# A blocked triangular inverse inside a two-block transformer kernel: corner products, narrower updates, masks on another engine

## What is computed

```python
decay = jnp.exp(jnp.where(causal, gc[..., :, None] - gc[..., None, :], -jnp.inf))
a_strict = jnp.where(idx[:, None] > idx[None, :],
                     jnp.einsum('bhncd,bhnsd->bhncs', k_beta, k) * decay, 0.0)
tri = a_strict + jnp.eye(c)
u = triangular_solve(tri, v * beta[..., None], lower=True, unit_diagonal=True)
w = triangular_solve(tri, k_beta * jnp.exp(gc)[..., None], lower=True, unit_diagonal=True)
```

## Time and profile before

| | us |
|---|---|
| median of 3 runs | 2701.99 |
| lowest, highest | 2698.80, 2703.09 |
| the profiled execution, its own time | 2697.01 |
| its span, first to last instruction | 2695.2 |
| PE busy, share of the span | 91% |
| DVE busy | 65% |
| ACT busy | 42% |
| POOL busy | 4% |
| mean granted PE clock, 1 is 2.4 GHz | 0.957 |

### The profile page before, as it was taken

One profiled execution on the slowest core, in us unless ns is written; L12 is line 12 of the kernel. 1 busy time (PEld: TensorE's weight loads), 2 busy tenths in 40 slices (PEclk: granted clock), 3 DMA queues, 4 the chain that ended last, 5 costly groups with the idle time before them and its releaser, 6 DMA issues. The chain is left out here.

```text
span 2695.2 us, 46289 instructions
## 1 busy us (share of the span) xinstructions
PE 2464.9 (91%) x18937; PEld 2367.2 (88%) x18937; DVE 1739.8 (65%) x2529; ACT 1120.7 (42%) x1600; POOL 103.2 (4%) x149
## 2 busy tenths in 40 slices
PE   6788679997986799989998999999999989999998
PEld 6788569997965699989998889899999988898998
DVE  4765357776383477757775575677777755756776
ACT  4542343333463333324334655533433346554332
POOL 2300000000000000000003000000000030000000
PEclk8999779998998699999999999999999999999999
DMA  7320135553911355534556223455364463234542
GB/s 198 122 79 17 35 109 188 187 187 105 221 43 51 104 177 180 180 109 164 180 172 161 94 95 110 157 172 187 131 197 162 151 172 99 94 119 163 180 162 80
DMA packets 294979, 370.17 MB, mean 137 GB/s; under 512 B 15321, under 2 KB 263634, under 8 KB 294802
## 3 DMA queue, kind: packets, MB, share of 16 engines
q1 hardware_dynamic: 289584, 354.85, 40.4%
q0 software_dynamic: 4880, 13.13, 2.7%
q10 hardware_dynamic: 370, 0.11, 0.0%
HBM read 360.20 MB, written 7.86 MB: 137 GB/s over the span
## 5 line engine op out<-in xcount | busy, mean ns | idle before, releaser
L302 PE MATMUL psum_banks<-source_high,weights_high 128*128 128x272 f32 (+1 forms) x3680 | 1080.4, 294 | 71.8 <-DVE weights_low L1540 21.3
L304 PE MATMUL psum_banks<-source_high,weights_low 128*128 128x272 f32 (+1 forms) x3680 | 1065.2, 289 | 0.0
L303 PE MATMUL psum_banks<-source_low,weights_high 128*128 128x272 f32 (+1 forms) x3680 | 1065.1, 289 | 0.0
L302 PEld LDWEIGHTS psum_banks<-source_high,weights_high 128*128 128x128 f32 x3680 | 710.6, 193 | 82.8 <-issue 24.3
L303 PEld LDWEIGHTS psum_banks<-source_low,weights_high 128*128 128x128 f32 x3680 | 711.2, 193 | 0.7
L304 PEld LDWEIGHTS psum_banks<-source_high,weights_low 128*128 128x128 f32 x3680 | 710.1, 193 | 0.0
L302 PE MATMUL psum_banks<-hidden_high,weights_high 128*128 128x272 f32 (+1 forms) x1216 | 349.8, 288 | 0.2 <-DVE h L1039 0.2
L304 PE MATMUL psum_banks<-hidden_high,weights_low 128*128 128x272 f32 (+1 forms) x1216 | 348.4, 287 | 0.0
L303 PE MATMUL psum_banks<-hidden_low,weights_high 128*128 128x272 f32 (+1 forms) x1216 | 347.3, 286 | 0.0
L1540 DVE TENSOR_TENSOR weights_low<-weight_ring,weights_high 128x2048 fp32r<-128x2048 f32 x102 | 234.1, 2297 | 174.0 <-ACT weights_high L1533 173.4
L1013 DVE TENSOR_TENSOR weights_low<-weight_ring,weights_high 128x2048 fp32r<-128x2048 f32 x131 | 292.9, 2287 | 74.0 <-ACT weights_high L1007 73.9
(11 more groups left out here) (403 smaller groups left out, 2902.8 us busy)
## 6 DMA issues: line engine op xcount, KB each, us to landing
weight_ring<-ffn_w_in SPq DMA_DIRECT2D x88, 1024.0 KB, 6.6
weight_ring<-w_in SPq DMA_DIRECT2D x48, 1024.0 KB, 5.3
weight_ring<-ffn_w_out SPq DMA_DIRECT2D x44, 1024.0 KB, 5.0
weight_ring<-moe_w_gate SPq DMA_DIRECT2D x32, 1024.0 KB, 6.8
weight_ring<-moe_w_up SPq DMA_DIRECT2D x32, 1024.0 KB, 7.6
weight_ring<-moe_w_down SPq DMA_DIRECT2D x32, 1024.0 KB, 5.0
weight_ring<-gdn_w_in SPq DMA_DIRECT2D x16, 1024.0 KB, 5.9
weight_ring<-w_branch SPq DMA_DIRECT2D x12, 1024.0 KB, 5.1
```

The costliest lines, as they stand in the source:

```text
L302: pe.matmul(out, w_hi, x_hi, start=start, stop=False)
L303: pe.matmul(out, w_hi, x_lo, start=False, stop=False)
L304: return pe.matmul(out, w_lo, x_hi, start=False, stop=stop)
```

## The change

Three edits are made in `gdn_layer`, all in the inverse.

1. In levels 0 to 4 a product of eight heads is made by `per_block`: for each head two products of 64x64 with 64 columns, one in rows and columns 0 to 63, one in rows and columns 64 to 127 of the array. Up to blocks of 64 nothing else of the 128x128 matrices is used. The last level keeps the full products.
2. DVE updates only what a level changes: in X the left block of each pair of blocks, in XT the right one, for each corner apart. This is four instructions on 64 partitions with 256 elements each, in place of two with 128x1024. The last level updates only columns 64 to 127 of XT, 128x512.
3. The masked matrices `pair` of levels 1 to 5 are made by POOL, and not by DVE between the products. They alternate between two pairs of buffers: levels 0, 2 and 4 use `temp`, levels 1, 3 and 5 use `spare`, which lies in `squares` and `raw`. POOL's mask for level 1 waits for the turned matrix of its chunk (the same event as `first(t)`), the masks for level 2 on wait until the first product of the level two before has been made. PE waits for `ready` before each first product from level 1 on.

```diff
-        half_step, pair = (A[:, 0], A[:, 1]), (temp[:, 0], temp[:, 1])
+        half_step = (A[:, 0], A[:, 1])
+        spare = [ap.rearrange("p n c -> p (n c)")[:, 0:H * P].rearrange("p (h c) -> p h c", h=H) for ap in (squares[:, :, :], raw[:, :, :])]
+        pair = ((temp[:, 0], temp[:, 1]), spare)
+        corner = [slice(0, P // 2), slice(P // 2, P)]
@@ gpsimd
+                for lev in range(1, LEVELS):
+                    for t in range(2):
+                        if lev == 1 and t == 0:
+                            pool.wait_ge(ss_mm.sem, ss_mm.at(GDN_V))
+                            pool.wait_ge(conv_n.sem, conv_n.at(GDN_Z))
+                        if lev == 1:
+                            pool.wait_ge(act_n.sem, act_n.at(A_AT + t))
+                        else:
+                            inv[t].begin(pool, 4 * (lev - 2) + 1)
+                        pool.tensor_tensor(pair[lev % 2][t], AT[:, t], pr.const(f"pairT{2 << lev}").unsqueeze(1).to_broadcast([P, H, P]), ALU.mult).then_inc(ready.sem, 1)
@@ tensor
+                def per_block(b, lhs, rhs):
+                    for h in range(H):
+                        for s in corner:
+                            ins = pe.matmul(bank2(b)[s, h, s], lhs(h)[s, s], rhs(h)[s, s], start=True, stop=True)
+                    return ins
+
                 for lev in range(LEVELS):
+                    product = per_block if lev < LEVELS - 1 else per_head
                     for t in range(2):
+                        L = pair[lev % 2][t]
                         if lev:
                             inv[t].begin(pe, 4 * lev)
+                            pe.wait_ge(ready.sem, ready.at(6 + 2 * lev + t - 1))
...
-                        inv[t].end(per_head(4 * t, lambda h: pair[t][:, h, :], lambda h: X[:, t, h, :]))
+                        inv[t].end(product(4 * t, lambda h: L[:, h, :], lambda h: X[:, t, h, :]))
...
-                            per_head(4 * t + 2, lambda h: XT[:, t, h, :], lambda h: half_step[t][:, h, :])
-                        inv[t].end(per_head(4 * t, lambda h: half_step[t][:, h, :], lambda h: XT[:, t, h, :]))
+                            product(4 * t + 2, lambda h: XT[:, t, h, :], lambda h: half_step[t][:, h, :])
+                        inv[t].end(product(4 * t, lambda h: half_step[t][:, h, :], lambda h: XT[:, t, h, :]))
@@ vector
-                    dve.tensor_tensor(pair[t], AT[:, t], mask("pairT2"), mul).then_inc(dve_n.sem, 1)
+                    dve.tensor_tensor(pair[0][t], AT[:, t], mask("pairT2"), mul).then_inc(dve_n.sem, 1)
...
+                def left(ap, s, b):
+                    return ap[s, :, s].rearrange("p h (m b) -> p h m b", b=2 * b)[:, :, :, 0:b]
+
+                def right(ap, s, b):
+                    return ap[s, :, s].rearrange("p h (m b) -> p h m b", b=2 * b)[:, :, :, b:2 * b]
...
-                            dve.tensor_tensor(pair[t], AT[:, t], mask(f"pairT{4 << lev}"), mul)
-                            dve.tensor_tensor(X[:, t], X[:, t], bank2(4 * t + 2), sub)
-                        inv[t].end(dve.tensor_tensor(XT[:, t], XT[:, t], bank2(4 * t), sub))
+                            b = 2 << lev
+                            for s in corner:
+                                x = left(X[:, t], s, b)
+                                dve.tensor_tensor(x, x, left(bank2(4 * t + 2), s, b), sub)
+                                x = right(XT[:, t], s, b)
+                                ins = dve.tensor_tensor(x, x, right(bank2(4 * t), s, b), sub)
+                            inv[t].end(ins)
+                        else:
+                            x = XT[:, t, :, P // 2:P]
+                            inv[t].end(dve.tensor_tensor(x, x, bank2(4 * t)[:, :, P // 2:P], sub))
```

More of the change, by code:

```diff
@@ L2063, in gdn_layer @@
     dve_n.passed(13)
-    ready.passed(6)
+    ready.passed(16)
     conv_n.passed(GDN_Z)
```

## The result

| us | before | changed |
|---|---|---|
| median | 2700.74 (2698.79 to 2703.67, 6 runs) | 2679.57 (2677.21 to 2683.20, 6 runs) |
| time of the profiled execution | 2697.01 | 2683.20 |
| its span | 2695.2 | 2681.4 |
| mean granted PE clock | 0.957 | 0.953 |

The changed kernel takes 0.9919 of the time of the kernel before it, with a 95% interval of 0.9908 to 0.9929: 21 us less, where the prediction had 25. The page's first line answers to the earlier trace rows; PE is as busy as before over the whole span, and POOL has 27 us more.

The account below looks back on a forecast made before the run. The prediction took the stage to be bound by a PE and DVE dependence ring, 12.78 us a level; 29.4 us gained less 4.2 for masks gave 25.2, so 2677 from 2702.0, chance 0.68, range 2667 to 2684, whole range to 2700.

Parts of the forecast that it names:

- Product, 0.96: Corner products of the inverse: two corners run at once, 60 ns a pair, 16 pairs, 0.96 us a product.
- corners in turns: Rival for the corner products: corners take turns, 1.92 us a product, period 11.5, kernel 2699.5, no change; chance 0.13.
- Update, 1.55 a chunk: DVE's four narrower update instructions for a chunk: 1.55 us in place of 3.5.
- Period, 6.71: One level of the inverse: five products of 0.96, 0.31, chunk 1's update of 1.55 and 0.05; PE's order binds.
- Slower: Rival: corners in turn, each record at the old 112 ns; product 3.58, period 19.8, kernel 2749; chance 0.07.
- Level 0 and level 5, 7.8 and 8.2: First and last level of the inverse: 7.8 us (5.1 less), first 4.0 at half clock, and 8.2 us (2.2 less).
- The masks at the start, +4.2: Start of the stage: POOL's two level 1 masks delay DVE's `first` chain by 2 x 2.1 = 4.2 us.
- POOL is not slowed: Where POOL masks and DVE instructions collide: only DVE is held up, 2.0 to 2.1 us a mask.
- Masks beside the updates, 0: Updates beside POOL's masks: 0 us taken, as they read one SBUF tensor; between 0 and 2.1 a mask possible.
- The side jobs, +2.2: DVE's side jobs after level 1: L2015 waits about 2.4 for POOL's mask, next update 2.6 late; 2.2 us more.
- The clock was a rival: Rival: PE stays at 1.2 GHz through the stage, products 1.92, stage 72.9, kernel 2704.6; chance 0.04.
- The gain passes on in full: After the stage: nothing is tied to a fixed time, weights lie ready, so the whole 25.2 us reaches the kernel.

Follow-up runs that it names:

- h_one_corner: Changed kernel with the second corner's products left out in levels 0 to 4 (output not the reference's): 2696.36 us, 1 run.
- j_x_first: Changed kernel with level 1's POOL masks and DVE's side jobs later, X updated before XT, and the next first product waiting for X alone: 2668.33 us, ratio 0.9877.
- b: Changed kernel, but DVE updates whole 64x64 corners, 512 elements an instruction instead of 256: 2690.42 us, ratio 0.9955.
- c: Changed kernel, but DVE makes the masks again, ahead of the updates, and POOL makes none: 2687.26 us, ratio 0.9939.
- f_both_later: Changed kernel with POOL's level 1 masks waiting for the end of first(1) and DVE's side jobs moved behind levels 3 and 4: 2672.39 us, ratio 0.9884.
- g: Changed kernel with no masks on POOL; DVE makes them in idle time ahead of use, side jobs behind levels 3 and 4: 2671.06 us, ratio 0.9885.
- k_filled: Changed kernel with masks on DVE ahead of the updates, plus chunk 0's first product repeated unread in levels 1 to 4: 2682.14 us, ratio 0.9929.
- d_masks_later: Changed kernel with POOL's masks for level 1 waiting for the end of first(1), not the turned matrix: 2674.21 us, ratio 0.9894.
- a: Changed kernel with full 128x128 products in levels 0 to 4 again, all else kept: 2696.04 us, ratio 0.9976.
- e_jobs_later: Changed kernel with DVE's side jobs moved: panel 17's low half behind level 3, scaling of z behind level 4: 2676.75 us, ratio 0.9904.
- after_again: The changed kernel, unedited, measured again beside the last experiments: 2681.31 us, ratio 0.9928.
- i: Changed kernel with products issued corner by corner, eight heads of one and then eight of the other: 2725.11 us, 1 run.

## Why the prediction was right, and where its terms were off

**Product, 0.96.** Measured 0.93. The mechanism, two corners at once, is right, as one corner against two at the same clock shows. The price is luck. It was taken from L2767 in the earlier trace rows, whose records have 64-column weights but stream 32 columns each, half of a corner's 64 (16x32 in the row), and the kernel issues four of them for one half and then four for the other. At the 0.83 ns a column of the same rows, 32 columns take 27 ns, so records 30 ns apart need no overlap at all. A corner's 64 columns take 53 ns by the same rate, and two corners at once give 53 a pair, where 58 was measured and 60 taken. By this rate, too, corners in turns would cost 1.7 a product and not 1.92; h_one_corner's 0.107 a record at 1.2 GHz says the same, as an estimate: half of that, 32 times, is 1.7.

The rule of the Trainium skill (TensorEngine Tiling (Array Packing), Restrictions and Gotchas), that different row tiles cannot access one PSUM bank simultaneously, was put by the prediction at 1.92 for this product and 2699.5 for the kernel. For diagonal corners, whose outputs lie on other partitions of the bank, the runs disagree with it.

**Update, 1.55 a chunk.** Measured 1.53: 0.41 each, 190.78 to 192.31, with one instruction held back where the half changes. Also runs of two elements at level 0, for which no row stood, cost nothing extra.

**Period, 6.71.** Measured 6.51, and PE's order with chunk 1's update is the bound as said: 5 x 0.93 + 0.31 + 1.53 + 0.05 = 6.54. j_x_first takes half of the update out of this loop, and another one, through ACT's copy, binds at 6.01. Two slips of the prediction changed nothing here: the terms of level 0 add to 7.67 and not 7.8, and in the rival *Slower* the period has six products, 6 x 3.58 = 21.5 and not 19.8, which is what its 43 us go by.

**Level 0 and level 5, 7.8 and 8.2.** Measured 6.9 and 8.1. The clock came back to 1.00 at 187.7, 2.1 us after the first weight load, not 4.0. That part was luck of the moment: in b, c, f, g, j and k it came 3.5 to 4.0 us after it, in d 1.3.

**The masks at the start, +4.2.** Measured +4.6 against the start before, and 4.3 by d_masks_later. The rest, 0.3, comes with the corner products: in a, the one version without them, the start is 13.9, and in the others PE's weight loads show 0.33 us idle ahead of the first corner. The mechanism of the 4.3 is the predicted one; two of the six instructions of `first` take the delay:

```profile
171.39 3.31 POOL L1677 TENSOR_TENSOR squares<-a_turned,consts_gdn 128x1024 f32<-128x1024 f32 x1 [61.14 <-ACT a_turned L1890]
...
172.40 3.39 DVE L1999 TENSOR_TENSOR inverse_pair<-a_turned,consts_gdn 128x1024 f32<-128x1024 f32 x1
174.66 3.33 POOL L1677 TENSOR_TENSOR qkv_padded<-a_turned,consts_gdn 128x1024 f32<-128x1024 f32 x1
175.71 3.35 DVE L2000 TENSOR_TENSOR temp<-a_turned,consts_gdn 128x1024 f32<-128x1024 f32 x1
```

"POOL is not slowed" was wrong for this place: its masks take 3.3 here and 2.36 alone.

**Masks beside the updates, 0.** Measured 0: POOL's two masks run from 187.62 on for 4.67 us, and the update at 190.78 lasts 0.41, as do all others. They read one tensor from SBUF and one from PSUM. The trace agrees here with the Trainium skill (SBUF — State Buffer, Who interferes with whom), by which a DVE instruction with at most one SBUF input, outside the two-port modes, does not contend with GpSimd.

**The side jobs, +2.2: the term that was mis-sized.** The loop took 46.8 where the terms of the prediction give 45.0, although the plain levels were shorter than foreseen. DVE between levels 2 and 3:

```profile
200.14 6.71 POOL L1677 TENSOR_TENSOR temp<-a_turned,consts_gdn 128x1024 f32<-128x1024 f32 x2 [1.83 <-PE psum_banks L1753]
...
200.72 3.93 DVE L1540 TENSOR_TENSOR weights_low<-weight_ring,weights_high 128x2048 fp32r<-128x2048 f32 x1
...
204.57 3.36 DVE L2050 TENSOR_SCALAR gate_z<-gate_z,params 128x2048 f32<-128x2048 f32 x1
...
207.94 0.41 DVE L2039 TENSOR_TENSOR inverse_pair<-inverse_pair,psum_banks 64x256 f32<-64x256 f32 x1
...
209.52 1.97 PE L1753 MATMUL psum_banks<-inverse_pair,squares 64*64 64x64 f32 x32 [3.90 <-DVE inverse_pair L2041]
```

The prediction let one mask catch one job. Both masks caught one each: the panel took 3.93 and not 2.29, the scaling 3.36 and not 1.28, so the two took 7.2 us from start to end, not 5.8. The next update was due at 197.30 + 6.51 = 203.8 and began at 207.9, 4.1 late instead of 2.6. The level took 10.57, 4.1 over the period. That much is a matter of size. The second part was no term at all: PE was idle for 3.90 us, the granted clock was 0.50 from 208.2 to 215.0, the products took 1.7 each, and the next level took 8.11, another 1.6. 4.1 + 1.6 = 5.7, which is what e_jobs_later took away. In after_again the first part is the same 4.1 (10.57 - 6.51), and the second 0.4 (6.88 - 6.51), as the stretch at 1.2 GHz is half as long. The prediction had 2.2, and its bound of 3.6 was passed both times. The clock was a rival there only for the whole stage. That a single late update would bring it down was not considered, and it came down behind it in both profiles of the changed kernel and in d, where level 3 takes 7.85.

**Why the total was near.** The misses offset each other in part: 0.8 less for four plain levels, 0.9 less for level 0, 0.1 for level 5 on one side, 3.5 more for the side jobs, 0.1 for level 4 and 0.4 at the start on the other. The stage gained 23.0 and not 25.2; that the misses nearly cancel is luck. The kernel gained 21.

**"The gain passes on in full."** Nearly. In nine of the eleven versions above that have a ratio, the time saved lies within 3 us of what the stage saved (a: 6.2 in the stage, 6.5 in the time; d: 27.8 and 28.4; f: 32.5 and 30.1; j: 34.6 and 34.1). The two others, both of the last series, saved less: k_filled 3.3, after_again 24.2 - 19.0 = 5.2. But the two profiled executions differ by 13.8 only. Of the missing 9 us, 2.5 were lost ahead of the stage: DVE's first instruction of `first(0)` starts at 168.72 in the kernel before and at 171.26 in the changed one. In the twelve later profiles it starts between 168.7 and 171.2, whatever the edit, so this is not the change. DVE's halving of the same weight panel starts at 418.55 in the kernel before and at 400.30 in the changed one, 18.3 earlier, and at 681.56 against 662.33, 19.2 earlier; near the end the same comparison (2603.19 against 2589.28) gives 13.9. What goes in between can be seen in windows of the same work, from the start of one weight panel's halving to that of a later one, the same two panels each time: the kernel before, the changed one, and the changed one again (after_again).

```profile
681.56:832.70 151.14, 133.81 (x1031) 115.43 (x1030) 88.72 (x147) 78.15 (x203) 2.23 (x2) 0.97 0.46 108
```

```profile
662.33:816.55 154.22, 138.09 (x1031) 118.86 (x1030) 88.79 (x146) 78.26 (x203) 2.23 (x2) 0.93 0.45 105
```

```profile
657.21:813.67 156.46, 138.12 (x1031) 119.29 (x1030) 88.71 (x146) 78.12 (x203) 2.23 (x2) 0.93 0.44 102
```

The same 1031 matmul records take 3.1 and 5.3 us more in the changed kernel, at a lower granted clock. A second such window (1214.39 to 1274.88 before) gives 1.7 and 1.6 more, with 0.95 before and 0.92 in both others. So the extra stretches at 1.2 GHz are in both profiles of the changed kernel. There is one profile only of the kernel before, but the mean granted clock is on record for more executions: 0.955 over the 26 of the kernel before beside the experiments, 0.951 over the ten of the changed one. That is, as an estimate, 20 us more at 1.2 GHz, of which 7 to 10 lie in the stage (13.7 and 17.1 in the two profiles against 6.8 before). What brings the rest is open, as e and f, with the same work behind the stage, have 0.954 and 0.955 over four executions each. In time it is little: the medians differ by 21.2 where the stage gives 23.0 in the first series, and by 19.0 where it gives 24.2 in the last.

## What to carry to other kernels

In a ring of dependences, work that is small against the period (a mask, a copy, a weight panel) belongs a whole period ahead of its use and beside nothing that it can slow; that was worth 9 us here (f_both_later against the changed kernel), nearly half as much as the change itself. Independent products on diagonal corners of the array have to alternate closely in the queue; here they do so after every product of one head, two records. And when an edit opens a gap in PE's work, look at the granted clock behind it before you cost the gap: it added 0.4 to 1.6 us behind a gap of 3.9, and 1.1 to 1.5 a level in c, whose gaps sum to 2.6.

## What the runs showed of the hardware

- Two 64x64 corners of the array, in other rows and other columns and writing one PSUM bank on other partitions, run at once: 32 records in 0.93 us at 2.4 GHz, and 1.71 for 32, 1.70 for 16 of one corner, at 1.2 GHz.
- They do so all along where the corners alternate after every two records. With 16 records of one and 16 of the other a product takes 2.68 at 1.2 GHz, and, worked out from that time, three or four records overlap at each change.
- PE busy for 10.00 us of 10.00 doesn't mean the high clock. With one corner, or one corner after the other, it was granted 0.50 for 65 us (h) and 96 us (i) on end. What of it is due to the half-used array, and what would bring the clock back, wasn't tried.
- Idle time of PE of 2.6 to 2.7 us in a period of 10 (c) went with 3.4 us at 1.2 GHz in each period; four products that nobody reads took both away and gave 5.4 us back, with 1.7 to 2.0 us of idle time left (k). With 2.3 us (b) the clock fell in levels 1 to 3 and stayed in level 4, so the idle time alone doesn't settle it.
- DVE and POOL take turns in all these rows when both read two SBUF tensors. The scaling of z (L2050) reads one SBUF tensor only and was caught too, 3.36 for 1.28. Its 2048 elements take 1.28 where L1540's 2048 take 2.29, so it runs at nearly twice the pace a column; the Trainium skill (SBUF — State Buffer, Who interferes with whom) has `tensor_scalar` in a two-port mode contend with GpSimd, and the trace agrees. A very small instruction waits for its turn too. L2053 works on 16 columns and lasted 0.17 in the kernel before (at 221.42 there, as L2018); behind a mask it lasted 2.34:

```profile
211.58 2.91 POOL L1677 TENSOR_TENSOR squares<-a_turned,consts_gdn 128x1024 f32<-128x1024 f32 x1 [4.74 <-PE psum_banks L1753]
...
212.19 2.34 DVE L2053 TENSOR_TENSOR decay_small<-decay_small 128x16 f32<-128x16 f32 x1
```

POOL is not free of it either: its mask takes 2.36 with no such DVE instruction beside it, 2.91 here, and 3.31 beside `first`.
